# Projection weights loaded once per pair of quarters, fewer expert matrices recast, the rest cast as they are loaded

## The reference, cut to what matters

```
proj = rmsnorm(x) @ w_in                 # 4384 columns: 1024 pooling, 3072 r/k/v, 288 low-rank
pool = causal windows 2/4/8/16 of proj[:, :1024], then a 256x256 map per group
z    = r/k/v and low-rank columns mixed with those of the token before (token shift)
y    = rwkv7(z): 16 heads of 64, state S_t = S_{t-1}(diag(w_t) + a_t b_t^T) + v_t k_t^T, y_t = S_t r_t
h    = x + concat(pool, y) @ w_out
h    = h + softmax(rmsnorm(h) @ w_q @ K^T) V @ w_o      # K, V from 256 memory tokens, 4 heads
h    = h + mixture of 16 SwiGLU experts (2048 -> 512 -> 2048), two experts of one group per token
out  = rmsnorm(h)
```

## Time and profile before

| | |
|---|---|
| time, median of 3 runs | 2645.34 us (2636.29 to 2829.83) |
| the profiled execution | 2657.1 us |
| its span (core 5, the slowest) | 2655.5 us |
| spans of the eight cores | 2600.4 to 2655.5 us |
| PE busy over the span | 2320.9 us, 87% |
| DVE, ACT, POOL busy | 52%, 47%, 13% |
| POOL transfers (software queue) | 251.00 MB, 63.7% of 16 DMA engines |
| SP transfers (hardware queue) | 172.62 MB, 21.2% |
| mean granted TensorE clock | 0.924 of full speed on core 5 |

### The profile page before, as it was taken

One profiled execution on the slowest core, in us unless ns is written; L12 is line 12 of the kernel. 1 busy time (PEld: TensorE's weight loads), 2 busy tenths in 40 slices (PEclk: granted clock), 3 DMA queues, 4 the chain that ended last, 5 costly groups with the idle time before them and its releaser, 6 DMA issues.

```text
span 2655.5 us, 57345 instructions; the slowest of 8 cores (2600.4 to 2655.5 us)
## 1 busy us (share of the span) xinstructions
PE 2320.9 (87%) x25144; PEld 1301.2 (49%) x25144; DVE 1387.1 (52%) x2599; ACT 1249.5 (47%) x2307; POOL 338.8 (13%) x555
## 2 busy tenths in 40 slices
PE   5898797877888978968998899999995999999975
PEld 3555454544445545534555455545553555555542
DVE  3545665555555655546667333333334466656633
ACT  5556584655755665645677333323332243433212
POOL 2011111111111112211110000000001011110211
PEclk9777898989889989989999899999997999999987
DMA  9798999888799789997995699999987568777893
GB/s 181 126 141 132 143 128 143 123 128 138 119 137 143 137 143 145 147 147 127 147 143 153 159 161 156 148 171 166 168 136 217 176 222 262 243 256 224 224 183 96
DMA packets 175296, 427.35 MB, mean 161 GB/s; under 512 B 80032, under 2 KB 101024, under 8 KB 160704
## 3 DMA queue, kind: packets, MB, share of 16 engines
q0 software_dynamic: 86288, 251.00, 63.7%
q1 hardware_dynamic: 88752, 172.62, 21.2%
HBM read 598.87 MB, written 142.74 MB: 279 GB/s over the span
## 4 chain that ended last, share of the span: by engine, by line
PE 69%; DMA 18%; DVE 5%; ACT 4%; issue 2%; POOL 0%; SPq 0%; POOLq 0%; DVEq 0%; ACTq 0%
PE ps L128 69%; ACT big L144 4%; DMA big<-x 3%; DMA big<-w_kv 3%; DVE big L151 3%; DMA qkd<-big 3%; DMA vod<-big 2%; DVE big L156 2%; DMA big<-w_qT 2%; DMA big<-w_o 1%; DMA big<-mixd 1%; DMA big<-h_s,big 1%; DMA big<-w_pl 1%; DMA h_s<-big 0%; DVE big L172 0%
## 5 line engine op out<-in xcount | busy, mean ns | idle before, releaser
L128 PE MATMUL ps<-big 64*64 64x64 bf16 (+8 forms) x25144 | 2320.9, 265 | 304.1 <-ACT big L144 88.3
L128 PEld LDWEIGHTS ps<-big 64*64 64x64 bf16 (+4 forms) x25144 | 1301.2, 110 | 1323.3 <-issue 215.8
L144 ACT ACTIVATE big<-ps 128x512 bf16<-128x512 f32 (+2 forms) x904 | 509.2, 588 | 860.6 <-PE ps L128 849.5
L151 DVE TENSOR_TENSOR big<-ps,big 128x512 bf16<-128x512 f32 (+3 forms) x656 | 466.3, 721 | 624.5 <-PE ps L128 449.9
L144 ACT ACTIVATE big<-big 128x512 f32<-128x512 f32 (+6 forms) x896 | 543.4, 633 | 314.4 <-DVE big L156 140.5
L144 ACT ACTIVATE big<-ps,big 128x512 f32<-128x512 f32 (+3 forms) x332 | 211.1, 648 | 202.2 <-PE ps L128 200.0
L156 DVE SCALAR_TENSOR_TENSOR big<-ps,big 128x512 f32<-128x512 f32 (+2 forms) x316 | 223.8, 721 | 142.2 <-ACT big L144 91.7
L156 DVE SCALAR_TENSOR_TENSOR big<-big 128x512 bf16<-128x512 f32 (+4 forms) x212 | 227.4, 1079 | 32.8 <-DMA big<-h_s,big 16.5
L151 DVE TENSOR_TENSOR big<-big 128x512 bf16<-128x512 f32 (+12 forms) x406 | 199.3, 512 | 57.8 <-ACT big L144 47.8
L156 DVE SCALAR_TENSOR_TENSOR big<-big,ps 128x64 f32<-128x64 f32 (+1 forms) x280 | 91.8, 331 | 154.4 <-PE ps L128 152.7
L172 DVE CAST big<-ps 128x512 bf16<-128x512 f32 x168 | 111.3, 686 | 57.6 <-ACT big L144 30.5
(11 more groups left out here) (27 smaller groups left out, 196.4 us busy)
## 6 DMA issues: line engine op xcount, KB each, us to landing
big<-w_rkv POOLq DMA_DIRECT2D x96, 512.0 KB, 11.6
big<-x SPq DMA_DIRECT2D x32, 1024.0 KB, 11.4
wgc<-wg_l POOLq DMA_DIRECT2D x56, 512.0 KB, 12.6
big<-wgc SPq DMA_DIRECT2D x56, 512.0 KB, 5.0
wuc<-wu_l POOLq DMA_DIRECT2D x52, 512.0 KB, 11.3
wdc<-wd_l POOLq DMA_DIRECT2D x52, 512.0 KB, 11.4
big<-wuc SPq DMA_DIRECT2D x52, 512.0 KB, 5.6
big<-wdc SPq DMA_DIRECT2D x52, 512.0 KB, 5.0
```

Source lines behind the costliest of these rows:

```text
L128: r.append(e.matmul(out, lhsT=lhsT, rhs=rhs, start=st, stop=sp_, **k))
L144: return self.op("act", lambda e: e.activation(out=out, in_=in_, func=func, **kw), dur, R, W, P, tbl=TBL.get(func))
L151: return self.op(eng, lambda e: e.tensor_tensor(out=out, in0=a, in1=b, op=op), dur, R, W, P)
```

## The change

- Projection tiles are loaded only where `q` is even and used for quarters `q` and `q + 1`; the units run in pairs of quarters (order list below); `wring` has eight buffers.
- The tiles 4 to 7 of x are normed with unit 0, tiles 8 to 15 at units 14 to 17; the square is written into the place in `hn` that the transposes fill later, and `xn1` goes. The low-rank weights go through `cw`, in four pieces each.
- `cw` has eight buffers of 128x512 in place of six of 128x1024, and `c_steps` loads pieces of half the size.
- `ERC` is 30 and `EXM` 14: 120 pieces are recast, 56 of them in the first stage, picked evenly over the experts (five of every eight pieces, in the order expert, part, matrix). The other 72 are cast as they are loaded.
- The planner's rate is 330 and counts DRAM ends only; matmuls of one accumulation are tied in order (`group`).
- The tiles of the second and third stage move to fit: `w_out` takes 4, 7 and 5 places where it had 4, 9 and 3.

```diff
-DMA_RATE = 480.0
+DMA_RATE = 330.0
...
+    def group(self, steps, b):
+
+        o = None
+        for items, R in steps:
+            o = self.mm(items, R=R, P=[b], after=[o] if o else ())
+        return o
...
-        nb = n * sum(4 if a.dtype == F32 else 2 for a in (out, in_))
+        nb = n * sum(4 if a.dtype == F32 else 2 for a in (out, in_) if a.space == "DRAM")
...
-EXM, ERC = 20, 40
+EXM, ERC = 14, 30
...
-        xt1, xn1 = m.f32(D), m.bf16(D)
+        xt1 = m.f32(D)
...
-        cw = m.bf16s(6, 1024)
+        cw = m.bf16s(8, 512)
...
-        wring = m.bf16s(6, 2048)
+        wring = m.bf16s(8, 2048)
...
-        pb_ = [m.f32(16 + QT) for _ in range(2)]
+        pb_ = m.f32(16 + QT)
...
-        first = [(a_.f32(D), a_.bf16(D)) for _ in range(3)]
+        a_ = Al(S, big, WORDS - 3 * D, WORDS)
+        first = [a_.f32(D) for _ in range(3)]
...
-            rstd_of(xt.a, xt, st, xn)
+            S.act(dst3, r3(xt.a, 16), AF.Square, R=[xt], P=[st, dbuf], accum_out=st.a[:, 0:1])
+            jk = S.ops[-1]
+            rstd_from(st)
...
-            xt, xn = first[i] if i < 3 else (xt1, xn1)
+            xt = first[i % 4] if i < 8 and i % 4 < 3 else xt1
...
             for bi, (c0, n) in enumerate(((0, 128), (128, 128), (256, 32))):
-                w_ = wring.next()
-                S.dma("pool", r3(w_.a, 16)[:, :, 0:n], wl3[:, :, c0:c0 + n], W=[w_])
-                b = proj(w_, r3(w_.a, 16), n, tq)
+                ws = [cw.next() for _ in range(4)]
+                for g in range(4):
+                    S.dma("pool", r3(ws[g].a, 4)[:, :, 0:n], wl3[:, 4 * g:4 * g + 4, c0:c0 + n], W=[ws[g]])
+                b = proj(ws, n, tq)
...
-            wb = wload(w_pl[r])
-            b = proj(wb, r3(wb.a, 16), 128, tq)
-            p = pb_[cc]
+            if tq % 2 == 0:
+                pws[r] = wload(w_pl[r])
+            b = proj(pws[r], 128, tq)
+            p = pb_.fresh()
...
-        units = [dict(hp=u % 8, q=u // 8) for u in range(32)]
+        pst, pws = {}, {}
+        order = [(q, h) for h in range(6) for q in (0, 1)] + [(0, 6), (0, 7), (1, 6), (1, 7), (2, 0), (2, 1), (3, 0), (3, 1)]
+        order += [(q, h) for h in range(2, 6) for q in (2, 3)] + [(2, 6), (2, 7), (3, 6), (3, 7)]
+        units = [dict(hp=h, q=q) for q, h in order]
...
-            U["w"] = [wload(w_rkv[t * 8 + hp]) for t in (1, 0, 2)]
+            if q % 2 == 0:
+                uw[hp] = [wload(w_rkv[t * 8 + hp]) for t in (1, 0, 2)]
...
-        ejobs = [(wec[k][e][c], wel[k][e][c], wed[k][e][c]) for e in range(16) for k in range(3) for c in range(4)][:ERC * 4]
+        ejobs = [(wec[k][e][c], wel[k][e][c], wed[k][e][c]) for e in range(16) for c in range(4) for k in range(3)]
+        ejobs = [j for n, j in enumerate(ejobs) if (n + 1) * ERC // 48 > n * ERC // 48]
...
+                            for g in range(4):
+                                w = cpiece(w_kv[t * 16 + h * 4 + jp * 2 + i][:, g * 512:(g + 1) * 512])
...
+                for c4 in range(4):
+                    ws = [cpiece(w_qT[(h * 4 + i) * 128:(h * 4 + i + 1) * 128, c4 * 512:(c4 + 1) * 512]) for i in range(4)]
...
-                    q, r = divmod(u, 8)
-                    if q < 3:
-                        if r in (2, 3, 4, 5):
-                            st_norm((q + 1) * 4 + r - 2)
-                        elif r == 6:
-                            st_lora(q + 1)
+
+                    for i in {0: range(4, 8), 14: (8, 9), 15: (10, 11), 16: (12, 13), 17: (14, 15)}.get(u, ()):
+                        st_norm(i)
+                    if u in (0, 15, 17):
+                        while held:
+                            held = next(cg, None)
+                            done += 1
+                        st_lora({0: 1, 15: 2, 17: 3}[u])
...
-            WP = [HN_OFF + i * 1024 for i in range(4)] + [AC_OFF + i * 1024 for i in range(9)] + [WR_OFF + i * 1024 for i in range(3)]
+            WP = [HN_OFF + i * 1024 for i in range(4)] + [AC_OFF + i * 1024 for i in range(7)] + [WR_OFF + i * 1024 for i in range(5)]
...
-                                                            bounds_check=BCV, oob_is_err=False), 1000.0, R=[idx] + h2d, W=yq, nbytes=1 << 21)
+                                                            bounds_check=BCV, oob_is_err=False), 1000.0, R=[idx] + h2d, W=yq, nbytes=1 << 20)
```

More of the change, by code:

```diff
@@ L591, in build @@
         vbr = m.bf16s(2, QT)
-        GLr = [m.f32s(2, 8) for _ in range(8)]
+        GLr = [m.f32s(3, 8) for _ in range(8)]
         Zc, Sc = [m.f32(64) for _ in range(8)], [m.bf16(64) for _ in range(8)]
+        bonr = m.f32s(2, QT)
         NBr, KBr = m.bf16s(2, 1024), m.bf16s(2, 1024)
@@ L886, in c_steps @@
             for i in range(2):
-                norm_tile(mem[i * 128:(i + 1) * 128, :], xt1, xn1, 48, mT3[:, :, i * 128:(i + 1) * 128], memT)
+                norm_tile(mem[i * 128:(i + 1) * 128, :], xt1, 48, mT3[:, :, i * 128:(i + 1) * 128], memT)
                 yield
@@ L895, in c_steps @@
                         b = pr.next()
+                        steps = []
                         for i in range(2):
[L897 to L901, removed]
+                            for g in range(4):
+                                w = cpiece(w_kv[t * 16 + h * 4 + jp * 2 + i][:, g * 512:(g + 1) * 512])
+                                w3 = r3(w.a, 4)
+                                steps.append(([(b.a[:, i * 256:(i + 1) * 256], w3[:, k, :], mT3[:, g * 4 + k, :], g + k == 0, g * 4 + k == 15) for k in range(4)], [w, memT]))
+                        S.group(steps, b)
                         evac(r3(KV.a, 4)[:, jp * 2:jp * 2 + 2, :], r3(b.a, 2), R=[b], P=[KV])
@@ L904, in c_steps @@
                 K3, V3 = r3(kv[0].a, 4), r3(kv[1].a, 4)
-                for half in range(2):
-                    ws = [cpiece(w_qT[(h * 4 + i) * 128:(h * 4 + i + 1) * 128, half * 1024:(half + 1) * 1024]) for i in range(4)]
-                    for cp_ in range(0, 8, 2):
+                for c4 in range(4):
+                    ws = [cpiece(w_qT[(h * 4 + i) * 128:(h * 4 + i + 1) * 128, c4 * 512:(c4 + 1) * 512]) for i in range(4)]
+                    for cp_ in range(0, 4, 2):
                         b = pr.next()
@@ L911, in c_steps @@
                             S.mm([(o_, ws[i].a[:, c * 128:(c + 1) * 128], K3[:, i, :], i == 0, i == 3) for i in range(4)], R=ws + [kv[0]], P=[b])
-                        c = half * 8 + cp_
+                        c = c4 * 4 + cp_
                         spill(b, qkd[:, h, c:c + 2, :], qkq[h], gc.a[:, c:c + 2])
-                        yield
-                for half in range(2):
-                    ws = [cpiece(w_o[(h * 4 + i) * 128:(h * 4 + i + 1) * 128, half * 1024:(half + 1) * 1024]) for i in range(4)]
+                        yield cp_ == 0
+                for db in range(4):
+                    ws = [cpiece(w_o[(h * 4 + i) * 128:(h * 4 + i + 1) * 128, db * 512:(db + 1) * 512]) for i in range(4)]
                     for mc in range(2):
[L918 to L921, removed]
-                            d0 = half * 1024 + db * 512
-                            spill(b, vod[:, h * 2 + mc, d0:d0 + 512], voq[h])
-                            yield
+                        b = pr.next()
+                        S.mm([(b.a, V3[:, i, mc * 128:(mc + 1) * 128], ws[i].a, i == 0, i == 3) for i in range(4)], R=ws + [kv[1]], W=[b])
+                        spill(b, vod[:, h * 2 + mc, db * 512:(db + 1) * 512], voq[h])
+                        yield mc == 0
         if stop >= 2:
@@ L939, in build @@
                 if u < 32:
-                    pool_piece(u, pst)
+                    pool_piece(order[u], pst)
                     st_prep(u)
-                    q, r = divmod(u, 8)
-                    if q < 3:
-                        if r in (2, 3, 4, 5):
-                            st_norm((q + 1) * 4 + r - 2)
-                        elif r == 6:
-                            st_lora(q + 1)
+                    for i in {0: range(4, 8), 14: (8, 9), 15: (10, 11), 16: (12, 13), 17: (14, 15)}.get(u, ()):
[5 more added lines that the diff above has]
+                        st_lora({0: 1, 15: 2, 17: 3}[u])
+                    if u == 0:
+                        for f_ in first:
+                            s_, e_, _ = next(r for r in S.regions if r[2] is f_)
+                            for s0, e0, o_ in S.regions:
+                                if s0 < e_ and s_ < e0 and o_ is not f_:
+                                    assert o_.w is None and not o_.p
+                                    o_.r += f_.users()
                     if stop >= 3:
                         while done < NS and done * 27 < NS * u:
-                            next(cg, None)
+                            held = next(cg, None)
                             done += 1
@@ L1301, in build @@
                         w3 = r3(w.a, 16)
-                        for kk in range(2):
```

(2 more changed lines are left out.)

52 lines of the change are left out of this document (27 added, 25 removed).

## The result

The changed kernel takes 2511.49 us (median of 4 runs, 2508.93 to 2514.63) against 2636.29 us (median of 3, 2624.80 to 2645.34) for the kernel before on the same chip: a ratio of 0.953, 95% interval 0.9481 to 0.958. It is faster by 125 us, where 177 (2645.34 to 2468) was forecast. Some executions of either kernel show a lower granted clock on one die and take some per cent longer; the times from here on leave them out, while the 2645.34 and the range of the kernel before, given ahead of the prediction, include one. The profiled execution took 2513.94 us, its span on the slowest core (again core 5) is 2512.3 us, and the page gives PE 91%, DVE 55%, ACT 49%, POOL 16%; the POOL queue moved 217.45 MB in place of 251.00.

The account below looks back on a forecast made before the run. Full DMA queues delaying small loads were taken to bound the first stage, PE the second. From 2657.1 us, -164 (first stage), -4 (second) and -10 (experts) gave 2479 profiled, 2468 median; range 2400 to 2530, chance 0.60.

Parts of the forecast that it names:

- The experts did not give it back: Rival, chance 0.12: in the experts DMA demand equals PE's time, +53 us in place of -10, about 2530 us.
- the smaller pieces did not land later: Rival, chance 0.06: smaller `cw` pieces mean more waits, about +151 us, 2795, if landing stays above some 10 us.
- the half-size pieces as a cost only: First stage: 164 added transfers, from halved pieces and split w_lo, cost 0 to 88 us of DMA work, 20 taken.
- The off-chain rival: Rival, chance 0.16: w_rkv is not on the chain, `cw` waits stay: -76 us, about 2570 (2540 to 2620).
- 60% of the idle time between start and end, -113: First stage: shorter queues remove 60% of PE's 188 us idle between start and end, -113 us (-47 to -188).
- +15 for the new order: First stage: waits for x at units 14 to 17, through `xt1` and `hn`, cost +15 us (0 to +40).
- a sign of being wrong that the prediction had named: First stage: x or w_lo waits of tens of us at units 14 to 18 would show the forecast wrong.
- The clock, -66: First stage: fewer PE pauses raise the clock; three quarters of 88 us on 128x512 matmuls, -66 us (0 to -88).
- The planner, in the range only: All queues: the planner's other rate reorders them; no row prices it, so it entered only the range.
- DMA demand, 1026 us: First stage: DMA work falls from 1320 us by 314, plus 20 for added transfers, to 1026, a share of 0.78.
- Second stage, -4: Second stage: 64 recasts in place of 80, 66 us less DMA, but PE covers it: -4 us (0 to -6).
- experts, -10: Experts: the last stretch is mended while the rest goes to nearly full DMA engines, -10 us (-26 to +53).

Follow-up runs that it names:

- 0.09 beyond: The changed kernel with no recast in the first stage, all 120 in the second: 2719.82 us, ratio 1.0321.
- start with two heads: The changed kernel with units beginning (0,0), (0,1), (1,0), (1,1) in place of (0,0), (1,0), (0,1), (1,1): 2513.59 us, ratio 0.9538.

## Why the prediction was right in sign and too large

The measured time lies inside the forecast's own range (2400 to 2530), near its upper end.

**What held.** The first stage was where the time came from, and loads that are not on the chain do delay work that is: giving the tile loads back costs 53 us. The experts did not give it back (623 against 632 on the median core), and the smaller pieces did not land later (5.8 us, where over 10 was to decide it).

**What is not shown.** Undone one at a time, loads 53, recasts 43 and planner 29 sum to 125 us, as much as the whole change gained. That match is luck: on the median core the three give back 67 of the 108 us of the first stage, and 20 us of the experts where the change gained 9. Some of the missing 41 can be the long profiled execution of the kernel before. The rest belongs to parts that were never undone alone (the half-size pieces of `cw`, the order of the units, `group`) or to what the parts do together; which of these stays open. The prediction counted the half-size pieces as a cost only. With the tile loads back they still land in 6.9 us, so they may be a gain.

**The off-chain rival** (2570) named the right doubt: undone in the changed kernel, relief was worth 0.18 us per us of DMA work by the loads, 0.17 by the recasts (115 us for 19), 0.09 beyond. The measured time lies between it and the forecast.

**The steps that were off, first of all sizes of the first stage (-164 forecast, -124 measured on core 5).**
- *60% of the idle time between start and end, -113, and +15 for the new order.* That is 98 us less; all idle time fell by 80. In the steady stretches only 5% is left, but the first 132 us went from 35 us idle to 45 (the row of the kernel before is the first below), and the turn at units 14 to 18 holds 43: the start was priced at 0, from x and the tiles alone and without the second set of w_lo (what that set costs was not tried), and the turn at +15. The second fence is the chain of the turn (start us, us, what); its 24 us of x and 10 of w_lo are a sign of being wrong that the prediction had named.
```profile
0.00:132.00 132.00, 96.70 (x887) 54.32 (x888) 58.75 (x129) 72.53 (x111) 24.64 (x45) 0.83 0.92 154
```
```profile
632.53 11.48 DMA big<-x
...
687.96 7.57 DMA big<-x
...
719.48 7.79 DMA big<-w_kv
...
735.79 8.39 DMA big<-w_kv
...
811.82 4.95 DMA big<-x
...
830.59 9.91 DMA big<-w_lo
```
- *The clock, -66.* PE's busy time fell by 44, for all shapes together. The price was wrong: matmul groups by shape, the first stage, then its steady stretch 264 to 594 us, where the clock is 0.99:
```profile
L128 PE MATMUL ps<-big 128*128 128x512 bf16 x2496 | 628.4, 384 | 16.1 <-DMA big<-w_lo 5.3 <-DVE big L158 4.1 <-DVE big L179 3.1
```
```profile
L128 PE MATMUL ps<-big 128*128 128x512 bf16 x680 | 170.1, 381 | 1.7 <-ACT big L151 1.3 <-DVE big L179 0.2
```
  628.4 / 2496 is 252 ns, and 170.1 / 680 is 250 at full clock, the 2.4 GHz level. So the 223 ns of the earlier trace rows are not reached here even at full clock, and most of the gap to 259 is not the clock's. The starts of the matmuls in the trace (core 5) show whose it is. A 128x512 matmul starts 216 ns (median) after one of its own shape in both stages, before and after. But the busy time of a group counts the last matmul of each run whole, 379 ns, though the next shape overlaps it (it starts after 309). In the steady stretch a run has 5.2 matmuls on average, in the earlier trace rows 24.2. With pauses left out, 4.2 starts of 220 ns and one of 379 make 250 ns each; 23.2 of 217 and one of 379 make 224. The prediction took the length of the runs for the clock; the clock's part was about 259 - 250 = 9 ns of the 35, some 22 us for this shape.
- *The planner, in the range only.* It is worth 29 us on the old kernel and 29 on the new one. Without it the rest of the change would have given about 100.
- *DMA demand, 1026 us.* It came out at 0.70 x 1359 = 951. The 112.57 MB on POOL are 214.7 pieces' worth at 58.9% of 1359 us, 3.73 us each where it was 3.84, and where the sum, with 867 us left for them, had 4.04: a piece took less of the engines' time than before, which the sum had not. The runs point to the queue's load as the reason: a recast, priced at 4.15, cost 4.8 us where 24 were put back (115 us) and 3.5 where 56 were taken out (194 us). They do not separate it from the other changes of these runs.
- *Second stage, -4, and experts, -10.* On core 5 they were 4 and 15, on the median core 16 and 9: in the second stage the profile's core hid what the others waited for.

## What to carry to other kernels

A transfer that is not on the chain can still be the cause of those that are, when all share full engines: look for small transfers that land later than large ones, then cut the large, and change the size of the small ones in a run of its own, since here most of their later landing went with something else. Price the gain with a falling rate (here, read in the changed kernel, 0.2 us per us of DMA work at a share of 0.8, 0.09 at 0.6), and take a matmul's price from the starts of neighbours, not from the busy time of its shape, which grows where the runs of one shape are short. Where a planner writes the order, its price of a transfer is part of the change; read a stage's length on all cores before calling it covered; and look in the trace whether an experiment moved what it was to move.

## What the runs showed of the hardware

- The share of busy engines alone does not set when a small transfer lands. On core 5 a 128 KB piece of w_kv landed in 5.8 us at a share of 0.70 and in 6.9 at 0.85; a 256 KB piece took 17.0 at 0.89 and 14.4 at 0.91 (the kernel before, with the planner of before and the new one). Size and order of the issues were not separated. 64 more transfers of the same bytes took about 0.3 us of the engines each.
- The cores of one chip, with the same program, ended the first stage 20 to 55 us apart: 22 in the changed kernel, 34 with its start with two heads at the same share of 0.70, 28 at 0.85, 32 and 54 at 0.90 and 0.89. The slowest core sets the time, and the change gained more there (1475 to 1354) than on the median core (1447 to 1339).
- At full clock a 128x512 bf16 matmul starts 216 ns (median) after one of its own shape, in the second stage of the changed kernel (1400 to 1880 us) as in its mixed first stage (264 to 594 us); a matmul of another shape starts 309 ns (median) after it in the mixed stage.
- In w_lo, rows of 2 KB in place of 512 B cut the packets of the POOL queue in the first stage from 81232 to 62800 at the same 112.57 MB and the DMA work by about 30 us of 942, and left the time as it was.
